# Two stacked transformer blocks on one Trainium2 core: index scores, the keys' norm and the weighted values moved, and the up products from the fifth unit on taken with 512 columns moving into the two halves of a PSUM bank

## What is computed

```
for l in range(2):                               # stages a0, a1
    proj = rms_norm(h) @ w_in                    # q,k,v, index q/k, conv, rwkv, gates
    y_a = dsa_attention(q, k, v, qi, ki, wi)     # top 64 of 256 keys by index scores
    y_b = short_conv_mixer(sc_u, sc_b, sc_c)
    y_c = rwkv7_time_mix(rw_z, ...)              # keys' norm kk / ||kk||, group norm of y
    h = h + sum(gates * up(y_a, y_b, y_c)) @ w_out
    u = causal_dwconv(rms_norm(h) @ w_up)        # w_up: 1024 x 5632
    h = h + (silu(gate(u)) * up(u)) @ w_down
for l in range(2):                               # stages b0, b1
    ya = dilated_mixture(q, k, v) * silu(z)      # 16 heads of 64
    yb = norm(diff_attention(...)) * silu(Z)     # 8 heads
    h = h + (sigmoid(g) * ya@pa + sigmoid(G) * yb@pb) @ w_out
out = rms_norm(h)
```

## Time and profile before

| | before |
|---|---|
| runs | 1700.82, 1702.55, 1703.81 us; median 1702.55 |
| the profiled execution, its own time | 1701.2 us |
| its span, first to last instruction | 1699.4 us |
| PE busy | 1668.6 us (98%), 13012 matmul records |
| DVE busy | 1166.9 us (69%) |
| ACT busy | 944.9 us (56%) |
| POOL busy | 196.2 us (12%) |
| mean granted clock of PE | 0.995 |
| read from HBM | 264.42 MB, 157 GB/s over the span |

### The profile page before, as it was taken

How to read it: one execution, slowest core, us unless ns; L and a number is a source line. 1 busy time by engine, 2 the same in 40 slices (tenths; PEclk the granted TensorE clock), 3 DMA queues, 4 the chain that set the end, 5 groups by cost and what they waited for, 6 DMA issues and landing times.

```text
span 1699.4 us, 30847 instructions
## 1 busy us (share of the span) xinstructions
PE 1668.6 (98%) x13012; PEld 1524.9 (90%) x13012; DVE 1166.9 (69%) x1624; ACT 944.9 (56%) x1397; POOL 196.2 (12%) x207
## 2 busy tenths in 40 slices
PE   7989999999999999999999999999999999999998
PEld 6979999999998989999999998887888988878887
DVE  7877456788778966548887775656766646567664
ACT  7474425655465484335554554665774556657743
POOL 0643500000002645200000000000000100000000
PEclk9999999999999999999999999999999999999999
DMA  7343532554545423424454544344345453344451
GB/s 272 138 148 106 165 123 100 199 193 177 182 163 180 168 100 132 162 101 174 149 203 175 182 190 174 127 146 165 133 164 184 168 200 127 141 162 145 152 195 50
DMA packets 48201, 268.24 MB, mean 158 GB/s; under 512 B 13568, under 2 KB 14464, under 8 KB 16448
## 3 DMA queue, kind: packets, MB, share of 16 engines
q1 hardware_dynamic: 38160, 263.65, 43.2%
q10 hardware_dynamic: 9136, 1.58, 0.5%
q0 software_dynamic: 768, 1.05, 0.3%
HBM read 264.42 MB, written 1.84 MB: 157 GB/s over the span
## 4 chain that ended last, share of the span: by engine, by line
PE 88%; DVE 7%; ACT 2%; POOL 1%; issue 1%; DMA 0%; DVEq 0%; SPq 0%; ACTq 0%
PE bank L1428 14%; PE bank L1429 14%; PE bank L1430 14%; PE bank L2543 10%; PE bank L2545 10%; PE bank L2544 10%; DVE w_low L938 3%; PE bank L2573 2%; DVE arena L1161 1%; PE bank L2614 1%; PE bank L2561 1%; ACT arena L654 1%; PE bank L1848 1%; DVE arena L1173 1%; PE bank L1687 1%; PE bank L1689 1%
## 5 line engine op out<-in xcount | busy, mean ns | idle before, releaser
L938 DVE TENSOR_TENSOR w_low<-slab,w_high 128x2048 fp32r<-128x2048 f32 x249 | 580.1, 2334 | 238.1 <-ACT w_high L578 231.0
L1428 PE MATMUL bank<-act_high,w_high 128*128 128x256 f32 (+1 forms) x2320 | 666.1, 287 | 0.1
L1429 PE MATMUL bank<-act_low,w_high 128*128 128x256 f32 (+1 forms) x2320 | 657.7, 283 | 0.0
L1430 PE MATMUL bank<-act_high,w_low 128*128 128x256 f32 (+1 forms) x2320 | 657.6, 283 | 0.0
L578 ACT ACTIVATE w_high<-slab 128x2048 fp32r<-128x2048 f32 x249 | 472.0, 1897 | 163.0 <-PE bank L2545 88.1
L1428 PEld LDWEIGHTS bank<-act_high,w_high 128*128 128x128 f32 (+1 forms) x2320 | 445.1, 192 | 8.8 <-issue 5.0
L1429 PEld LDWEIGHTS bank<-act_low,w_high 128*128 128x128 f32 (+1 forms) x2320 | 445.1, 192 | 0.9 <-issue 0.5
L1430 PEld LDWEIGHTS bank<-act_high,w_low 128*128 128x128 f32 (+1 forms) x2320 | 445.1, 192 | 0.1
L2543 PE MATMUL bank<-w_high,act_high 128*128 128x512 f32 x768 | 306.0, 398 | 0.0
L2545 PE MATMUL bank<-w_low,act_high 128*128 128x512 f32 x768 | 300.7, 391 | 0.0
L2544 PE MATMUL bank<-w_high,act_low 128*128 128x512 f32 x768 | 299.8, 390 | 0.0
(11 more groups left out here) (245 smaller groups left out, 1640.7 us busy)
## 6 DMA issues: line engine op xcount, KB each, us to landing
slab<-stream_a SPq DMA_DIRECT2D x143, 1024.0 KB, 4.8
slab<-stream_b SPq DMA_DIRECT2D x104, 1024.0 KB, 4.8
residual<-x_t SPq DMA_DIRECT2D x4, 256.0 KB, 5.8
slab<-stream_a ACTq DMA_DIRECT2D x2, 512.0 KB, 5.5
lora_weights<-lora SPq DMA_DIRECT2D x2, 512.0 KB, 8.0
out_t<-residual SPq DMA_DIRECT2D x4, 256.0 KB, 2.4
d_inverse<-arena POOLq DMA_DIRECT2D x2, 256.0 KB, 4.4
constants<-common SPq DMA_DIRECT2D x1, 384.0 KB, 8.5
```

The lines of the kernel that those rows point to most:

```text
L938: line.did(line.eng.tensor_tensor(core.wl[u % PARTS][:, 0:SLAB_WIDTH[u]], core.slab[u % SLABS][:, 0:SLAB_WIDTH[u]], core.wh[u % PARTS][:, ...
L1428: eng.matmul(out, wh, xh, start=first, stop=False, skip_group_check=True)
L1429: eng.matmul(out, wh, xl, start=False, stop=False, skip_group_check=True)
L1430: return eng.matmul(out, wl, xh, start=False, stop=last, skip_group_check=True)
```

## The change

It has five parts.

1. **Up units.** `NARROW_UP = 4`: from the fifth up unit of each layer on (18 of 22), one matmul with the high weight takes high and low activations together as 512 moving columns, into the two halves of one bank, and a second adds the low weight's product to the first half. The two activation tensors become one. The unit fills two banks (0 and 1, or 2 and 7 in turn). ACT copies the second halves out (128 x 512), DVE adds them to the first halves, and then scales by the token norm.
2. **Index scores and top 64.** `isc` 0 to 3 go from after `rz` 0 and 1 into their middle; each `topk` part goes one unit earlier.
3. **Keys' norm.** kk, its square, sum and root go from the `uc` units to `rz` 3 to 6; the sigmoid of the gate input goes from `lora_inputs` behind `lora`. After `gn` part 0 stands a load of the root's table.
4. **Weighted values** in b, first kind: DVE divides the softmax numerators before they are turned (`dve_share`), `pv` is made of four matmuls with 64 columns of v as the stationary operand (`pe_weighted`), so that the output is already turned and DVE only copies it. Instead of the outputs, z is turned (`z_turn`), one block per unit.
5. **In b**, `turn_late` (PE's `turn` at the end of its unit's steps) is used for the first of the second kind too, and in b0 the sums of squares are taken in two halves, after `v` 0 and in the middle of `v` 1.

```
+NARROW_UP = 4
...
-        self.xh = sb("act_high", [P, 16, T], F32R)
-        self.xl = sb("act_low", [P, 16, T], F32R)
+        self.x = sb("act", [P, 2, 16, T], F32R)
+        self.xh, self.xl = self.x[:, 0], self.x[:, 1]
...
+        if kind == "up" and i >= NARROW_UP:
+            b = 2 * (i % 2)
+            freed[b, reader] = freed.get((b, reader), 0) + 1
+            banks, fills = [(b, reader, freed[b, reader])], 0
...
-    put(("rz", 0), ("isc", 0), ("isc", 1))
-    put(("rz", 1), ("isc", 2), ("isc", 3))
+    amid(("rz", 0), ("isc", 0), ("isc", 1))
+    amid(("rz", 1), ("isc", 2), ("isc", 3))
     put(("rz", 2), ("turns", 2), ("turns", 3))
     for part in range(4):
-        put(("rz", 2 + part), ("topk", part))
+        put(("rz", 1 + part), ("topk", part))
+    put(("rz", 3), ("kk", 0))
+    put(("rz", 4), ("kk_square", 0))
+    put(("rz", 5), ("kk_sum", 0))
+    put(("rz", 6), ("kk_root", 0))
...
-        put(unit, ("scan_y", c), *([("scan_rhs", c + 1)] if c < NCH - 1 else [("gn", 0)]))
+        put(unit, ("scan_y", c), *([("scan_rhs", c + 1)] if c < NCH - 1 else [("gn", 0), ("root_table", 0)]))
...
-            late = (kind, n) == (0, 2)
+            late = n == 2
...
-    mid = {("v", 1): [("sum", 0), ("norm", 0)]}
+    mid = {("v", 1): [("sum", 1 if first else 0), ("norm", 0)]}
+    if first:
+        put(("v", 0), ("sum", 0))
...
+                made(core, eng, rows, UA["up", j])
+                rest = core.wide[rows[UA["up", j]][4][0][0]][:].rearrange("p (j n t) -> p j n t", j=2, n=2)[:, :, 1]
+                act(core.a(REST_ + 2 * (j % 2), 2), rest, ACT.Copy, sem("rest_copied"))
+            eng.wait_ge(*sem("up_scaled").next(eng))
...
+                parts = core.wide[b][:].rearrange("p (j n t) -> p j n t", j=2, n=2)
+                eng.wait_ge(*sem("rest_copied").next(eng))
+                did(tt(up, parts[:, :, 0], core.a(REST_ + 2 * (j % 2), 2), ALU.add), sem(f"dve_emptied{b}"))
+                line.settled()
+                did(tt(up, up, scale, ALU.mult), sem("up_scaled"))
...
+    def wide_product(u, j, k):
+        wh, wl = (w[(first + u) % PARTS][:].rearrange("p (k j m) -> p k j m", k=8, j=2) for w in (core.wh, core.wl))
+        at, out = inputs["up"](rows[u][1], k), core.bank[up_banks(u)[j]]
+        eng.matmul(out[:].rearrange("p (n t) -> p n t", n=2), wh[:, k, j, :], core.x[:, :, at, :], start=k == 0, stop=False,
+                   skip_group_check=True)
+        return eng.matmul(out[:, 0:T], wl[:, k, j, :], core.xh[:, at, :], start=False, stop=k == 7, skip_group_check=True)
...
+def pe_weighted(eng, out, p_t, value):
+    blocks = p_t.rearrange("p (n t) -> p n t", t=P)
+    for s in range(2):
+        for p in range(2):
+            o, v = out[HD * p:HD * p + HD], value(s, p)
+            if s == 0:
+                ins = eng.matmul(o[:, 0:T].rearrange("p (m t) -> p m t", m=2), v, blocks[:, p:2 * p + 3:2 + p], start=True, stop=False,
+                                 skip_group_check=True)
+            else:
+                ins = eng.matmul(o[:, P:T], v, blocks[:, 3 + 2 * p], start=False, stop=True, skip_group_check=True)
+    return ins
```

More of the change, by code:

```diff
@@ L197, in __init__ @@
         bank = lambda name, n=512: ctx.enter_context(nc.psum_tensor(name, [P, n], F32))
-        first, self.pair, self.pair2 = [bank(f"bank{i}") for i in range(3)], bank("bank3", 1024), bank("bank5", 1024)
-        self.bank = first + [pair[:, 512 * i:512 * i + 512] for pair in (self.pair, self.pair2) for i in range(2)] + [bank("bank7")]
+        self.wide = {0: bank("bank0", 1024), 2: bank("bank2", 1024)}
+        self.pair, self.pair2 = bank("bank3", 1024), bank("bank5", 1024)
+        self.bank = [pair[:, 512 * i:512 * i + 512] for pair in (self.wide[0], self.wide[2], self.pair, self.pair2) for i in range(2)]
+        self.bank.append(self.bank.pop(3))
         self.d_blocks = nc.dram_tensor("d_blocks", (8, 16, SUB, SUB), F32, kind="Internal").ap()
@@ L315 @@
[L315 to L319, removed]
@@ L486, in schedule_b @@
     put(("V", 1), ("silu", 0))
-    put(("V", 3), ("y", 0), ("y", 1), ("y", 2), ("y", 3))
-    for i, unit in enumerate((("Q", 0), ("Q", 1), ("K", 0), ("K", 1))):
-        put(unit, ("post", i))
+    for i, unit in enumerate((("V", 2), ("V", 3), ("Q", 0), ("Q", 1), ("K", 0))):
+        if i < 4:
+            put(unit, ("z_turn", i), ("y", i))
+        if i:
+            put(unit, ("post", i - 1))
     put(("g", 1), ("silu", 1))
@@ L984, in dve_normed, with dve_share @@
                                            op0=ALU.mult, op1=ALU.mult), tally)
+def dve_share(core, line, k, buf, tally):
+    rden = core.small[:, RDEN_:RDEN_ + 4]
+    line.settled()
+    line.did(line.eng.reciprocal(rden, core.small[:, DEN_ + 4 * (k % 4):][:, 0:4]))
+    line.settled()
+    for m in range(2):
+        part = buf[:, :, SPAN[m]]
+        line.did(line.eng.tensor_tensor(part, part, rden[:, 2 * m:2 * m + 2].unsqueeze(2).broadcast_to([P, 2, WIDTH[m]]), ALU.mult),
+                 tally if m else None)
+def pe_weighted(eng, out, p_t, value):
[9 more added lines that the diff above has]
+    return ins
 def vector_a(core, eng, line, stage):
@@ L1470, in product, with up_banks, up @@
         return gemm(eng, out, (wh[:, k, j, :], wl[:, k, j, :]), (core.xh[:, at, :], core.xl[:, at, :]), start, stop)
+    def up_banks(u):
+        b = rows[u][4][0][0]
+        return b, {0: 1, 2: 7}[b]
+    def wide_product(u, j, k):
[4 more added lines that the diff above has]
+        return eng.matmul(out[:, 0:T], wl[:, k, j, :], core.xh[:, at, :], start=False, stop=k == 7, skip_group_check=True)
+    def up(u):
+        eng.wait_ge(sem("slab_split").sem, first + u + 1)
+        b, partner = up_banks(u)
+        banks.free(partner)
+        banks.fill(b, "dve")
+        banks.held[partner] = banks.held[b]
+        for j in range(2):
+            for k in range(8):
+                last = wide_product(u, j, k)
+        last.then_inc(sem("products").sem, 1)
     def down(u):
@@ L1525, in unit @@
             return down(u)
+        if kind == "up" and i >= NARROW_UP:
+            return up(u)
         if (kind, i) in (("br2", 0), ("out", 0), ("up", 0)):
@@ L1566, in pe_square_pairs, with step @@
 def pe_square_pairs(core, eng, banks):
-    def step(_):
-        banks.held_for(7, "rooted_sums", 2)
-        for at in range(KD):
+    def step(part):
+        if part == 0:
+            banks.held_for(7, "rooted_sums", 2)
+        for at in range(4 * part, 4 * part + 4):
             if at % 2 == 0:
@@ L2277, in post @@
         kind, i = n // 4, n % 4
-        eng.wait_ge(*sem("outputs_turned").next(eng))
         at = 8 * (1 - kind) + 2 * i
-        scale = core.small[:, LAM_ + 1:LAM_ + 2] if kind else 1.0
-        act(core.xh[:, at:at + 2, :], heads(bank[6 + i % 2], T), ACT.Copy, sem("y_high"), scale=scale)
+        if kind:
+            eng.wait_ge(*sem("outputs_turned").upto(n + 1))
+            act(core.xh[:, at:at + 2, :], heads(bank[6 + i % 2], T), ACT.Copy, sem("y_high"), scale=core.small[:, LAM_ + 1:LAM_ + 2])
+        else:
+            eng.wait_ge(*sem("outputs_gated").upto(n + 1))
+            act(core.xh[:, at:at + 2, :], core.a(BO_ + 2 * i, 2), ACT.Copy, sem("y_high"))
     def gate(g):
@@ L2444, in y @@
         kind, i = n // 4, n % 4
+        if kind == 0:
+            eng.wait_ge(*sem("outputs_turned").upto(n + 1))
+            if n == 0:
+                line.settled()
+            o = core.a(BO_ + 2 * i, 2)
+            did(tt(o, heads(bank[6 + i % 2], T), o, ALU.mult), sem(f"dve_emptied{6 + i % 2}"))
+            line.tell(sem("outputs_gated"))
+            return
         if i == 0:
-            eng.wait_ge(*sem("z_ready").next(eng))
+            eng.wait_ge(*sem("z_ready").upto(2))
         if n == 4:
@@ L2468, in post @@
                     op1=ALU.subtract), sem(f"dve_emptied{b}"))
+            line.tell(sem("y_low"))
         else:
-            did(tt(low, heads(bank[b], T), high, ALU.subtract), sem(f"dve_emptied{b}"))
-        line.tell(sem("y_low"))
+            did(tt(low, core.a(BO_ + 2 * i, 2), high, ALU.subtract), sem("y_low"))
     def merge(i):
```

93 lines of the change are left out of this document (52 added, 41 removed).

## The result

Four runs of the changed kernel took 1689.91 to 1690.39 us, median **1690.07**; four runs of the kernel before, beside them, 1700.82 to 1703.81, median 1702.64. The ratio is 0.9927, its 95% interval 0.991 to 0.9945: faster by 0.7%, 12.6 us. The forecast was 1680. The profiled execution took 1690.39 us with a span of 1688.6; against the profiled execution before (span 1699.4) it is 10.8 us shorter.

A forecast was written before the change was run, and what follows sets the result against it. PE bounds the kernel, busy 1668.6 of 1699.4 us. Seven terms (−7.7 −5.4 −2.2 −5.7 −1.8 −3.2 +3.2) give −22.8; from 1701.2, plus 1.35 for the median, 1679.7, said as 1680; range 1665 to 1692.

The forecast's parts named there:

- the first rival: Whole kernel: waits move to later work on DVE and the half-clock stretches stay; 1690.5 us, chance 0.25.
- Part 1: FFN up units, 18 of 22 per layer: a unit takes 5.55 us in place of 5.76; −7.7 us.
- a case whose mechanism did not come: High end of the range, 1692 us: waits move, clock stays, with table losses; the case's chance 0.25.
- A removed matmul saves 13.3 ns: Wide up units: two matmuls of 256 columns cost 240.0 ns, one of 512 costs 226.7.
- The banks are no limit: Wide up units: a bank pair is refilled after over 11 us and emptied in about 1.3.
- the additions cost nothing: FFN: ACT's bank copy (0.60 us) and DVE's second pass (0.68) are hidden, with 0.7 us cover left per cycle.
- Part 2: Weighted values in b, 16 times: 0.34 us saved each, −5.4 us; bounds −6.9 to +6.6.
- Part 3: `turn` of the second kind at the unit's end in b: both waits for `combine` go, −2.2 us.
- part 4: Keys' norm, moved from uc units to rz 3 to 6: waits in lines 1801 and 1752 go, −5.7 us.
- part 5: Index scores and top 64 earlier: 0.9 us per layer off the wait for line 1188, −1.8 us.
- Part 6: Clock: two of three half-clock stretches of 3.4 us go, −3.2 us; bounds 0 and −4.8.
- Part 7: Group norm: the root's table load delays split and reciprocal by 1.5 to 1.6 us, twice; +3.2 us.

The follow-up runs named there:

- experiment 9: Changed kernel plus swapped bank pairs and no root-table load, with the two matmuls of a wide pair in turned order for every second k: 1675.75 us.
- experiment 8: Changed kernel with the weighted values' four matmuls grouped by output half in the program, not alternating: 1690.67 us.
- experiment 1: Changed kernel with the two pairs of banks of the wide up units swapped: median 1684.93 us, ratio to the kernel before 0.9902.
- experiment 6: Changed kernel with swapped bank pairs, plus PE waiting for its own last product ahead of each pair of wide up units: span 1691.1 us.
- experiment 7: Changed kernel with the keys' norm (kk, square, sum, root) back in the uc units: 1695.06 us.
- experiment 4: Changed kernel with index scores and top 64 back at their old places, keys' norm left at its new ones: median 1695.32 us.
- experiment 3: Changed kernel with no wide up unit (NARROW_UP = 22): median 1686.75 us.
- experiment 2: Changed kernel without the load of the root's table behind part 0 of the group norm: median 1685.85 us.

## Why the prediction was right, and where it was off

The range held the time and the direction was right. But the forecast was 10 us too low, and the time equals the first rival's 1690.5 only by its number: that rival said that waits move and the clock stretches stay. They did not stay; all three went, and two others came. That the range held the time is in part luck: part 1 was off by 10.1 us, and 1690.07 is inside because the upper end had been set by a case whose mechanism did not come.

- **Part 1, −7.7, measured +2.4.** This is the step that failed, in three places. "A removed matmul saves 13.3 ns" was a sum of two uniform streams (240.0 against 226.7). In the mixed stream it was 6.7 in 32 of 36 units (the first pair of each layer did reach 13.3), and experiment 9 got 4.7 of the missing 6.6 back by the order of sizes alone. The Trainium skill's rule (page "TensorE: Matmul & The Clock Gate", section "Back-to-back issue gap") would have given an estimate of 2.5; the 6.7 of the traces lie between it and my sum. "The banks are no limit" looked at the steady state alone: true there, false for the first wide unit, whose bank had been filled by the unit right ahead. It cost 5.1 us. And "the additions cost nothing" held in the cycles, as forecast, but not at the FFN's end, where DVE's lateness has nothing behind it to hide it: 1.4 us.
- **Part 2, −5.4, measured −5.7.** Right. The reason given, column groups side by side, is what the records show, also in experiment 8. Bounds of +6.6 were far too wide.
- **Part 3, −2.2, measured −2.7.** Right.
- **Parts 4 and 5, −7.5 in all.** In a0 4.87 us, in a1 about 1.7 beside the clock: 6.6. The sum was near, its division was not: undone alone, part 5 is worth 1.0 to 1.5 a layer and part 4 about 0.8, and what the two have together beyond that is not assigned. PE did then wait for `w_low` in the rz units, as foreseen.
- **Part 6, −3.2.** Three stretches went (−4.8) and two came (+3.2), so −1.6. One reading was off: the second stretch, from 609.34 on in a1, comes 1.8 us behind a wait of 1.8 in front of line 1752 (607.59), and the wait in front of the head sums was 0.28 there.
- **Part 7, +3.2, measured +3.1.** The wait grew by 1.5 us each, as worked out. The half clock behind it, the +3.2 of part 6, wasn't counted; with it the group norm costs 6.3. Part 6 should have asked for both signs.

Left open: why the wide stream has two rhythms, 346.7 and 353.3 ns, and which of them a pair of units takes. A stop ahead, the bank and the place alone don't decide it (experiments 1, 6, 7 and 8). Open too is what makes the clock fall behind one wait and not behind the same wait in another kernel.

## What to carry to other kernels

When a stage changes the form of its buffers in mid-course, check the first and the last use apart from the steady state: who holds the buffer at the seam, and what is late when the stage ends. Price a matmul by rows of the same mix of sizes, not of uniform streams, and put equal sizes next to each other. Where a change adds a wait of 2 us or so to PE, count a possible half-clock stretch on top. And do not add up the worth of two moves that ease the same engine.

## What the runs showed of the hardware

- Matmuls onto 64 output partitions each ran beside each other even when the program had them grouped by half: starts of the two halves 14 ns apart, 0.81 us for the group in either order, and the start order wasn't the program's.
- One stream, two exact rhythms: 512 + 256 columns in 346.7 or 353.3 ns, constant through both units of a pair; 348.8 in alternating order.
- The granted clock fell to 0.50 for 3.4 us (6.8 in experiment 4) behind some PE waits of 2 us and not behind others: behind the group norm's 2.27 us in both layers of the changed kernel, in one layer of experiments 3, 6 and 8 and in none of 1 and 4; behind the bank wait in one layer of experiments 2 and 7 and in none of the changed kernel. Each costs about 1.6 us, which is as much as most of the parts judged here.
- Where POOL and DVE were at work at once, one of the two rows could grow by about the other's length: in a0 a split of 2.29 us took 3.37 (at 83.12) while POOL was at its 128 x 512 products of 1.04 to 1.35, and such a product, 1.09 us elsewhere, took 3.42 (at 68.93) beside a split that kept its 2.28.
